# Four elementwise products of the second scan direction moved from VectorE to GpSimd in a hybrid trunk kernel

## The reference, cut to what matters

```python
for d in range(2):
    w = -jax.nn.softplus(-(f('rwkv_w0')[d] + jnp.tanh(xw) @ f('rwkv_w_up')[d])) - 0.5
    decay = jnp.exp(-jnp.exp(w))
    a = jax.nn.sigmoid(f('rwkv_a0')[d] + xa @ f('rwkv_a_up')[d])
    kd = hs(k * (1.0 + (a - 1.0) * f('rwkv_k_a')))
    yd, Sd = rwkv_scan(rh, hs(decay), kd, vh, kk, hs(a), s0[:, d], reverse=(d == 1))

def step(S, inp):
    r_t, w_t, k_t, v_t, kk_t, a_t = inp
    sa = jnp.einsum('bhij,bhj->bhi', S, -kk_t)
    S = (S * w_t[:, :, None, :] + sa[..., None] * (kk_t * a_t)[:, :, None, :]
         + v_t[..., None] * k_t[:, :, None, :])
    return S, jnp.einsum('bhij,bhj->bhi', S, r_t)
```

## Time and profile before

| what | value |
|---|---|
| time, median of 3 runs | 3039.5 us (3037.28 to 3039.64) |
| the profiled execution's own time | 3043.78 us |
| its span | 3041.7 us |
| instructions | 44609 |
| TensorE matmul busy | 2816.1 us, 93% |
| VectorE busy | 1618.8 us, 53% |
| ScalarE busy | 1100.1 us, 36% |
| GpSimd busy | 167.4 us, 6%, 209 instructions |
| mean granted TensorE clock | 0.958 of full speed |

### The profile page before, as it was taken

One profiled execution on the slowest core, in us unless ns is written; L12 is line 12 of the kernel. 1 busy time (PEld: TensorE's weight loads), 2 busy tenths in 40 slices (PEclk: granted clock), 3 DMA queues, 4 the chain that ended last, 5 costly groups with the idle time before them and its releaser, 6 DMA issues. The chain is left out here.

```text
span 3041.7 us, 44609 instructions
## 1 busy us (share of the span) xinstructions
PE 2816.1 (93%) x17315; PEld 2163.5 (71%) x17315; DVE 1618.8 (53%) x2108; ACT 1100.1 (36%) x1431; POOL 167.4 (6%) x209
## 2 busy tenths in 40 slices
PE   6899888899899999999968998888979999999997
PEld 1588655577677777778856786555768888888885
DVE  0465555545555555555545655555455555555555
ACT  0344322223433333333424442222344444444442
POOL 1000022200000000000000001112000000000000
PEclk9999998889999999999988998898989999999998
DMA  9765666655477777777634555666636666666662
GB/s 365 252 186 154 211 229 230 224 168 166 135 232 236 233 230 239 237 230 219 186 108 130 164 158 192 224 229 225 213 105 193 187 188 190 187 188 186 191 187 90
DMA packets 317248, 600.68 MB, mean 197 GB/s; under 512 B 23184, under 2 KB 29288, under 8 KB 316584
## 3 DMA queue, kind: packets, MB, share of 16 engines
q1 hardware_dynamic: 309488, 592.90, 62.4%
q10 hardware_dynamic: 7608, 5.60, 0.6%
HBM read 595.28 MB, written 3.15 MB: 197 GB/s over the span
## 5 line engine op out<-in xcount | busy, mean ns | idle before, releaser
L835 PE MATMUL bank<-hiW,actH 128*128 128x512 f32 (+1 forms) x2304 | 902.1, 392 | 4.0 <-DVE loW L1428 2.3
L835 PE MATMUL bank<-loW,actH 128*128 128x512 f32 (+1 forms) x2304 | 892.4, 387 | 0.0
L835 PE MATMUL bank<-hiW,actL 128*128 128x512 f32 (+1 forms) x2304 | 892.3, 387 | 0.0
L1345 DVE TENSOR_TENSOR loW<-rawW,hiW 128x1024 fp32r<-128x1024 f32 x348 | 425.7, 1225 | 429.2 <-ACT hiW L409 429.0
L409 ACT ACTIVATE hiW<-rawW 128x1024 fp32r<-128x1024 f32 x348 | 368.1, 1060 | 552.1 <-PE bank L835 552.1
L835 PEld LDWEIGHTS bank<-hiW,actH 128*128 128x128 f32 x2304 | 435.1, 189 | 113.9 <-issue 21.1
L835 PEld LDWEIGHTS bank<-hiW,actL 128*128 128x128 f32 x2304 | 434.3, 189 | 88.8
L835 PEld LDWEIGHTS bank<-loW,actH 128*128 128x128 f32 x2304 | 435.0, 189 | 86.5 <-issue 1.0
L1745 DVE TENSOR_TENSOR loW<-rawW,hiW 128x1024 fp32r<-128x1024 f32 x244 | 299.0, 1225 | 337.9 <-ACT hiW L644 337.7
L644 ACT ACTIVATE hiW<-rawW 128x1024 fp32r<-128x1024 f32 x244 | 258.7, 1060 | 447.9 <-PE bank L835 422.3
L835 PE MATMUL bank<-rawW,csR 128*32 128x512 f32 x1536 | 269.2, 634 | 29.3 <-DMA rawW<-in_w_ada 28.6
(11 more groups left out here) (254 smaller groups left out, 2260.6 us busy)
## 6 DMA issues: line engine op xcount, KB each, us to landing
rawW<-in_w_ada SPq DMA_DIRECT2D x384, 512.0 KB, 6.2
rawW<-in_w_gate SPq DMA_DIRECT2D x176, 512.0 KB, 3.7
rawW<-in_w_up SPq DMA_DIRECT2D x176, 512.0 KB, 3.7
rawW<-in_w_down SPq DMA_DIRECT2D x176, 512.0 KB, 3.7
rawW<-in_w_in SPq DMA_DIRECT2D x144, 512.0 KB, 3.6
rawW<-in_w_out SPq DMA_DIRECT2D x64, 512.0 KB, 3.7
rawW<-in_w_in SPq DMA_DIRECT2D x16, 160.0 KB, 2.3
x<-in_x_prompt SPq DMA_DIRECT2D x1, 1024.0 KB, 6.6
```

The costliest lines, as they stand in the source:

```text
L835: return pe.matmul(out, a, b, start=start, stop=stop, skip_group_check=True)
L1345: TT(loW[:, slot, :, 0:width], rawW[:, slot, :, 0:width], hiW[:, c % LEAD, :, 0:width].bitcast(F32), ALU.subtract).then_inc(lo_ready, 1)
```

## The change

In each pass GpSimd makes the four products of direction 1, and VectorE keeps those of direction 0. A new semaphore `rw_bk` tells GpSimd that both raw `be` are written, a new one `rw_kp` tells TensorE and VectorE that the four products are there. TensorE waits for `rw_kr` before direction 0 and for `rw_kp` before direction 1. VectorE waits for `rw_kp` ahead of the products `bg0`, which read `be` and `ga` of both directions. The two raw `be` products no longer count in VectorE's step counter, whose number goes from 27 to 25.

```diff
-VSTEPS, FSTEPS = 68, 27
+VSTEPS, FSTEPS = 68, 25
...
+        rw_bk, rw_kp = sem("rw_bk"), sem("rw_kp")
...
                         pool.tensor_copy(X[:, d, :, 0:HALF], unit)
 
+                    pool.wait_ge(rw_bk, it + 1)
+                    pool.wait_ge(rw_E, it + 1)
+                    settle(pool)
+                    pool.tensor_tensor(be[:, 1], be[:, 1], E1[:, 1, :, 0:128], ALU.mult)
+                    pool.tensor_tensor(KR[:, 1, :, 0], kk[:], E2[:, 1, :, 1:129], ALU.mult)
+                    pool.tensor_tensor(KR[:, 1, :, 1], rkv[:, 0], E2[:, 1, :, 0:128], ALU.mult)
+                    pool.tensor_tensor(ga[:, 1], kd[:, 1], E1[:, 1, :, 0:128], ALU.mult).then_inc(rw_kp, 1)
                     for d in range(2):
                         pool.wait_ge(rw_mA, it * 2 + (d + 1))
...
                     for d in range(2):
-                        pe.wait_ge(rw_kr, it * 2 + (d + 1))
+                        pe.wait_ge((rw_kr, rw_kp)[d], it + 1)
...
                     for d in range(2):
-                        R.mark(TT(flat(be[:, d]), flat(kk[:]), aa[d], ALU.mult))
-                    R.sync()
+                        e = TT(flat(be[:, d]), flat(kk[:]), aa[d], ALU.mult)
+                    e.then_inc(rw_bk, 1)
+                    dve.wait_ge(rw_bk, it + 1)
                     dve.wait_ge(rw_E, it + 1)
-                    for d in range(2):
-                        Ei, Ex, Ev = ((E1[:, d, :, 1:129], E1[:, d, :, 0:128], E2[:, d, :, 1:129]) if d == 0 else
-                                      (E2[:, d, :, 0:128], E2[:, d, :, 1:129], E1[:, d, :, 0:128]))
+                    for d in range(1):
+                        Ei, Ex, Ev = E1[:, d, :, 1:129], E1[:, d, :, 0:128], E2[:, d, :, 1:129]
...
                     TT(nrm[:], nrm[:], ksq[:], ALU.mult).then_inc(rw_bo, 1)
+                    dve.wait_ge(rw_kp, it + 1)
                     for d, end in ((0, E1[:, 0, 0, 128:129]), (1, E2[:, 1, 0, 0:1])):
```

## The result

The changed kernel takes 3056.3 us (3052.55 to 3057.58, 5 runs), the kernel before 3038.21 beside it (3037.28 to 3039.64). The ratio is 1.0053, 95% interval 1.0041 to 1.0066: slower by 18.1 us, where 13.8 were forecast.

The account below looks back on a forecast made before the run. The RWKV passes were taken as bound by a chain through VectorE and TensorE, not the stream. Moved products 0, turns 12.8 and clock 1 make 13.8 us over the median 3039.5: 3053.3 us, range 3042 to 3064.

Parts of the forecast that it names:

- What the moved products are worth: Taking four products (1.34 us per pass) off VectorE gains 0 on the path, as TensorE's direction 0 covers them.
- Taking turns: VectorE's second to fourth products of direction 0 each wait behind a GpSimd product: 1.6 us per pass, 12.8 in all.
- 0.87 to 1.35 named as a sign: Sign that the forecast is right: each of GpSimd's four products takes between 0.87 and 1.35 us.
- 4.8 was named: Sign that the forecast is right: TensorE's wait for VectorE's last product of direction 0 is 4.8 us in a pass.
- the rival's test by its start alone: Test of VectorE keeping the port: whether its second product starts 0.34 us after the first or 0.87.
- GpSimd's fourth product is covered by 1.3 us: GpSimd's last product ends near 449.5, TensorE asks for direction 1 only at 450.9, so that wait is covered.
- The clock, +1 us: TensorE's longer pause before direction 0 lowers its clock in some of five other passes: half of +2 us taken.
- bounds of -10 to +8.5: Limits of the clock term in us: five other passes at -2.0 each or at +1.7 each.
- No blocking: Rival, chance 0.05: VectorE's and GpSimd's products do not block each other; 3039.5 us, no change.
- VectorE keeps its turn: Rival, chance 0.09: VectorE's four back-to-back products keep the shared port; 0.1 us a pass, 3040.3 us in all.
- The clock repays: Rival, chance 0.08: five other passes gain 2.0 us each from the clock; 3042.3 us.
- The clock makes the pause dear: Rival, chance 0.14: five other passes lose 1.7 us each to the clock, over the 12.8; 3060.8 us.

Follow-up runs that it names:

- e1_after_turn: Changed kernel with GpSimd also waiting for `rw_kr`, so its four products start only after VectorE's four of direction 0: 3041.45 us, ratio 0.9995.
- e2: Kernel before plus four unused GpSimd products of constants per pass, which read SBUF beside VectorE's products: 3060.53 us, ratio 1.0058.
- e3: Kernel before plus two GpSimd memsets per pass, which only write SBUF, beside VectorE's products: 3041.15 us, ratio 1.0000.
- e4: Kernel before plus one unused VectorE reciprocal of 128x220 per pass ahead of direction 0's products, no GpSimd work added: 3056.88 us, ratio 1.0049.
- e8_order: Kernel before with ScalarE copying gT and making S0s, exponentials signalled per direction, direction 1's raw be after direction 0's products: 3032.75 us, ratio 0.9980.
- e11_order_fill: e8_order plus matmuls of constants in two TensorE pauses, four before the masked products and two before the levels: 3007.09 us, ratio 0.9900.
- e12_after_all_fill: Changed kernel with constant matmuls in three TensorE pauses: four of 512 columns before direction 0, four and two of 256 before masked products and levels: 3020.44 us.

## Why the prediction was right, and where its sizes were off

**What the moved products are worth: 0.** Right. In e1_after_turn they are off VectorE, and the time is that of before. They were covered by TensorE's direction 0 on either engine.

**Taking turns, 3 x 0.53 = 1.6 us per pass, 12.8 in all.** Right in mechanism and place, slightly too high: 1.50 us in all eight passes, 12.0 us. The row that it came from, L1630 at 0.95 us, is met within 0.05 by L1616 to L1618. e2 and e3 show that it is a collision of reads and nothing in the change's own structure. GpSimd's products took 0.79 to 0.90 us, a little under the 0.87 to 1.35 named as a sign, and TensorE's wait for L1618 was 20.1 / 4 = 5.0 us a pass where 4.8 was named. L1616 starts 0.34 us after L1615 and lasts 0.90: the rival's test by its start alone would have misled, since the record counts the blocked time as part of the instruction. The 0.83 us from its start to the next one decides.

**GpSimd's fourth product is covered by 1.3 us.** Right, and in pass 2 by more: 3.0 us, as direction 0 itself ran mostly at 1.2 GHz. With the 1.86 us that direction 0 took at the full clock it would have been 1.5. No TensorE wait for GpSimd appears.

**The clock, +1 us.** This is the term that failed in size. I took it that the five other passes might fall into the low state and would then cost 0.4 us each on balance. All five fell. Stretch C cost 8.1 us, and only 4.3 us came back in D and E, so the balance is +3.8 us inside the passes, within the bounds of -10 to +8.5, but four times the value taken. The same delay in e2 and e4 cost +6.9 and +7.3 us in these stretches, while e1 and e3, without it, stand at +1.5 and 0. So the term is more than +1 us in three profiles of three, and its size, some 4 to 7 us, is known no better than that. Three passes of one profile were too few for a mean of a quantity that ran from -2.0 to +1.7. Inside the passes the forecast of 13.8 us thus meets 17.2: -0.8 from the turns, +2.8 from the clock, +1.4 in A, where the sum had nothing. (e1 and e3 have 1.5 and 1.2 us more in A too, at the time of before, so A isn't shown to be a cost of the change.) The medians differ by 18.1; the 0.9 more, and the 4 us less of the two profiled executions, are spread of the executions or lie outside of the passes, which stays open.

**The rivals.** "No blocking" and "VectorE keeps its turn" fell with L1616 to L1618. "The clock repays" happened in part and never enough. "The clock makes the pause dear" was the one nearest to the truth beside the forecast: 3060.8 us against 3056.3.

## What to carry to other kernels

Before a piece of VectorE work is shared with GpSimd, find out whether both would read SBUF at once in the stretch that sets the start of TensorE; here one wait that put GpSimd behind VectorE turned a loss of 18 us into none. Look for VectorE instructions that last longer than others of their shape: that is where a collision hides, as no wait is recorded for it. And look at the granted clock behind each pause of TensorE: in this kernel two pauses of 1.8 and about 1 us in a pass went before levels that took 28.1 us, and with matmuls of constants in them the levels took 25.0. These matmuls, with a shorter path ahead of TensorE, won 31 us.

## What was not expected

- **Filling short pauses speeds up what comes behind.** Six small matmuls of constants per pass, in time that TensorE had spent idle, took the levels from a mean of 28.1 us (e8_order) to 25.0 us (e11_order_fill), the granted clock being 1.00 in all eight passes. e12_after_all_fill shows the same in the changed kernel (25.0 us).
- **Matmuls with 32 columns differed threefold in price.** The chunks' matmuls, which write four strips of a bank in turn, took 3.22 us for twelve, 0.27 us each; the filler, which always writes strip 0, 7.03 us for eight, 0.88 us each, at the full clock. That the strips are the reason was not tried.
- **A delay cost more than its length.** 1.5 us per pass, 12 in all, cost 14 (e4_delay) to 18 us (the change, e2_extra_reads); only e4's interval reaches below 12. The profiles put the rest into what the clock takes in one stretch and gives back in another. 0.7 us per pass cost about 5 us; its interval of 0.3 to 8.8 us can't tell whether a short delay is cheaper in proportion.
